# Three plain up-projection pairs in place of four, and the operands' preparation packed into six evacuations

## What is computed

```python
D_MODEL, D_FF = 1024, 2816

def swiglu(h, w_up, w_down):
    gate, up = jnp.split(h @ w_up, 2, axis=-1)
    return (jax.nn.silu(gate) * up) @ w_down

# in trunk():
h = rmsnorm(x, norm_ffn[l]) * (1.0 + sc2) + sh2
x = x + g2 * swiglu(h, w_up[l], w_down[l])
```

## Time and profile before

| | |
|---|---|
| runs, us | 939.48, 940.05, 941.44; median 940.05 |
| profiled execution, us | 940.5 |
| its span in the profile, us | 938.7 |
| granted TensorE clock | 0.995 of full speed (2.4 GHz) |
| busy, us | PE 915.1, PEld 887.8, DVE 672.3, ACT 446.5, POOL 107.6 |

### The profile page before, as it was taken

How to read it: one execution, slowest core, us unless ns; L and a number is a source line. 1 busy time by engine, 2 the same in 40 slices (tenths; PEclk the granted TensorE clock), 3 DMA queues, 4 the chain that set the end, 5 groups by cost and what they waited for, 6 DMA issues and landing times.

```text
span 938.7 us, 22364 instructions
## 1 busy us (share of the span) xinstructions
PE 915.1 (97%) x9385; PEld 887.8 (95%) x9385; DVE 672.3 (72%) x1254; ACT 446.5 (48%) x824; POOL 107.6 (11%) x135
## 2 busy tenths in 40 slices
PE   5999999999999999999999999999999999999997
PEld 4899988998999999999999999999999999999996
DVE  4778878866567677477766888999334999994454
ACT  6687445423334544753223257466213666663223
POOL 0110011112020110100100002122001322220000
PEclk8999999999999999999999999999999999999999
DMA  9834233443343422325643332332323433323212
GB/s 348 272 83 141 60 98 112 117 128 108 111 119 103 124 86 69 102 61 177 195 144 93 91 90 69 90 91 79 93 86 105 113 111 92 91 80 101 85 51 96
DMA packets 146030, 104.80 MB, mean 112 GB/s; under 512 B 5153, under 2 KB 138855, under 8 KB 144779
## 3 DMA queue, kind: packets, MB, share of 16 engines
q1 hardware_dynamic: 138955, 79.16, 28.8%
q0 software_dynamic: 6352, 22.00, 7.5%
q10 hardware_dynamic: 624, 2.23, 0.7%
HBM read 100.06 MB, written 3.31 MB: 110 GB/s over the span
## 4 chain that ended last, share of the span: by engine, by line
PE 90%; ACT 3%; DVE 3%; issue 2%; DMA 1%; SPq 1%; ACTq 0%; DVEq 0%
PE G L2225 59%; PE G L2320 19%; PE R L2233 10%; PE R L2236 1%; DMA wada<-in_w_ada_s 1%; SPq L1112 1%; DVE acc L1858 0%; DVE w_sum L1761 0%; DVE sum_lo L1770 0%; ACT L1244 0%; ACT L1283 0%; ACT inp L1283 0%; ACT w_hi L1267 0%; ACT rn L1295 0%; DVE cy L1893 0%
## 5 line engine op out<-in xcount | busy, mean ns | idle before, releaser
L2225 PE MATMUL G<-h_hi,w_hi 128*128 128x272 f32 (+1 forms) x880 | 263.4, 299 | 0.9 <-DVE w_lo L1654 0.7
L2225 PE MATMUL G<-h_lo,w_hi 128*128 128x272 f32 (+1 forms) x880 | 253.8, 288 | 0.0
L2225 PE MATMUL G<-h_hi,w_lo 128*128 128x272 f32 (+1 forms) x880 | 253.4, 288 | 0.0
L1654 DVE TENSOR_TENSOR w_lo<-raw,w_hi 128x1024 fp32r<-128x1024 f32 (+3 forms) x111 | 118.7, 1070 | 81.6 <-ACT w_hi L1267 80.5
L2225 PEld LDWEIGHTS G<-h_hi,w_hi 128*128 128x128 f32 x880 | 165.7, 188 | 4.2 <-issue 1.1
L2225 PEld LDWEIGHTS G<-h_lo,w_hi 128*128 128x128 f32 x880 | 166.0, 189 | 0.2 <-issue 0.2
L2225 PEld LDWEIGHTS G<-h_hi,w_lo 128*128 128x128 f32 x880 | 165.7, 188 | 0.0
L1267 ACT ACTIVATE w_hi<-raw 128x1024 fp32r<-128x1024 f32 (+3 forms) x111 | 101.5, 914 | 113.9 <-PE G L2225 113.6
L2320 PE MATMUL G<-x_hi,sum_hi 128*128 128x272 f32 x288 | 83.7, 291 | 1.5 <-ACT partial L1378 1.5
L2320 PE MATMUL G<-x_hi,sum_lo 128*128 128x272 f32 x288 | 83.4, 290 | 0.0
L2320 PE MATMUL G<-x_lo,sum_hi 128*128 128x272 f32 x288 | 83.1, 288 | 0.0
(11 more groups left out here) (335 smaller groups left out, 2111.7 us busy)
## 6 DMA issues: line engine op xcount, KB each, us to landing
raw<-in_w_in SPq DMA_DIRECT2D x48, 512.0 KB, 4.0
raw<-in_w_up SPq DMA_DIRECT2D x44, 512.0 KB, 3.9
w_ada<-in_w_ada_t POOLq DMA_DIRECT2D x49, 256.0 KB, 3.0
wada<-in_w_ada_s SPq DMA_DIRECT2D x8, 1024.0 KB, 13.4
raw<-in_w_down SPq DMA_DIRECT2D x14, 384.0 KB, 3.4
raw<-in_w_down SPq DMA_DIRECT2D x16, 320.0 KB, 3.1
raw<-in_w_out SPq DMA_DIRECT2D x8, 512.0 KB, 4.0
w_ada_t<-in_w_ada_t POOLq DMA_DIRECT2D x15, 256.0 KB, 3.2
```

Source lines behind the costliest of these rows:

```text
L1654: dve.tensor_tensor(lo, raw[:, i % RAW, 0:job.nk, 0:job.m], hi.bitcast(F32), ALU.subtract).then_inc(w_lo_done, 1)
L2225: ins = pe.matmul(out, w, x, start=(job.first and k == 0 and p == 0), stop=(job.last and k == job.nk - 1 and p == 2))
```

## The change

`PLAIN` becomes 3: tile 3 is made by a unit, the first run has seven units (tiles 3 to 9), and there are nineteen in all. The plain jobs have six evacuations in place of eight, and the preparation of the activation operands and of the first unit's weights is distributed over them anew. What no longer goes there, the high part of `T4` and the low parts of `B21` and `T4`, goes into the first unit's `rest`.

```diff
--- before.py
+++ after.py
@@ -54,7 +54,7 @@
 PACK = 2 * N_CHUNK
 LAST_SMALL = 4
 STAGES = 4
-PLAIN = 4
+PLAIN = 3
 PART = 10
 KP = KD // 2
 DOWN_K = (KF - PART) // 2
@@ -451,12 +451,10 @@
     rest = {n: [] for n in range(len(evac))}
     sums, high, low = prepare(0)
     rest[0] = [("x_hi", B11)]
-    rest[1] = [("x_sum", NT2), ("x_lo", B11), ("up_mul", 0)]
-    rest[2] = [("x_hi", NT1), ("x_shift", B21), ("x_sum", T3), ("x_lo", NT1), ("x_hi", B22)]
-    rest[3] = [("up_mul", 1), ("x_hi", NT2), ("x_sum", T4), ("x_lo", B22), ("x_hi", T3)]
-    rest[4] = [("x_hi", B21), ("x_lo", NT2), ("x_lo", T3), ("x_hi", T4)]
-    rest[5] = [sums[0], ("up_mul", 2), sums[1], ("x_lo", B21), *sums[2:]]
-    rest[6] = [*high[1:], ("x_lo", T4), low[0]]
+    rest[1] = [("x_sum", NT2), ("x_lo", B11), ("up_mul", 0), ("x_hi", NT1)]
+    rest[2] = [("x_shift", B21), ("x_sum", T3), ("x_lo", NT1), ("x_hi", B22), ("x_hi", NT2), ("x_lo", B22)]
+    rest[3] = [("up_mul", 1), ("x_sum", T4), sums[0], ("x_lo", NT2), sums[1], ("x_hi", T3), *sums[2:]]
+    rest[4] = [*high[1:], ("x_hi", B21), ("x_lo", T3), low[0]]
     del plan[mark:]
     plan.append(("duo", u0, u0 + 1))
     for n, one in enumerate(evac):
@@ -475,7 +473,7 @@
         if n + 2 < len(evac):
             plan.append(("split_lo", i))
         plan.extend(rest[n])
-    quick_run(range(PLAIN, PART), [("up_mul", PLAIN - 1), *low[1:]])
+    quick_run(range(PLAIN, PART), [("x_hi", T4), ("x_lo", B21), ("up_mul", PLAIN - 1), *low[1:], ("x_lo", T4)])
     for m in range(KD):
         add("down_a", m, [dict(w=t["w_down"][k0 * P:(k0 + nk) * P, m * P:(m + 1) * P].rearrange("(k p) m -> p k m", p=P),
                                nk=nk, src="a", k0=k0) for k0, nk in ((0, PART // 2), (PART // 2, PART // 2))])
```

## The result

| | before | after |
|---|---|---|
| median of 12 runs, us | 940.15 | 942.97 |
| lowest to highest | 937.59 to 943.02 | 942.01 to 946.29 |
| profiled execution, its span | 940.5, 938.7 | 944.08, 942.3 |

The medians are 2.8 us apart; the ratio is 1.0040, 95% interval 1.0029 to 1.0051, which is 3.8 us (2.7 to 4.8): slower, by more than the 0.2% that can be told apart. The runs of after lie in two groups, seven from 942.01 to 942.99, which hold the median, and five from 944.08 to 946.29, of which the profiled one is the lowest. Forecast were 942.5, a range of 940.4 to 944.7, and slower with a chance of 0.57. So it came out as forecast, but one of the terms was too small and one wasn't thought of; the rows show both.

What follows compares the result with a forecast made beforehand. TensorE is full overall, but DVE, preparing operands, ends last around the first unit. Saving - 1.43, old losses - 2.0, first unit + 5.0, later units + 0.9 give + 2.5 us: 942.5, range 940.4 to 944.7.

Steps and rivals of the forecast that it cites:

- Saving: On TensorE, a pair of 96 matmuls becomes a unit of 84: 12.14 less 10.71, 1.43 us saved.
- DVE ends last: Around the first unit, DVE finishes last and TensorE waits for it; DVE busy over 90% between 572 and 600.
- The rule weighed in the prediction: Whole kernel: work first on the engine with highest occupancy, TensorE; the sum would end at - 1.43 us.
- Three places: First unit's first product waits for `w_lo`, fifth for `sum_lo` of the third sum, seventh for `partial`; unit 14 to 16 us.
- The walk along DVE's queue: From 571.61 to the first unit's seventh product: start at 599.4 to 601.2, taken as 600.3, a 5.0 us loss.
- Wait (1): Fifth job's weights: DVE waits 0.58 us for ACT's `w_hi`, which comes later because `x_hi` is rounded first.
- wait (3): DVE's wait of 1.45 us at 603.01 stays, as ACT still rounds the last pair's result ahead of that sum.
- Wait (2): At `x_lo` of `B22`: DVE waits 1.17 us for ACT; POOL's two early sums fall largely there, minus 1.83.
- Later units: Units after the first in the first run: their old losses of 1.05 and 0.73 us half stay, 0.9.
- The packing also cures the old waits: First run of units: early sums and ready activations leave no waits; - 3.4 us, 936.6; chance 0.04.
- TensorE bounds after all: First run of units: old losses of 2.0 us stay and 1.43 is saved; 938.6; chance 0.06.
- A heavy loss: First units: DVE's waits mostly stay, later units lose as before; + 3.5 to + 5.6 us; chance 0.12.

Runs made afterwards that it cites:

- e5_four: Kernel before, four plain pairs kept, with six steps moved: four of ScalarE's and two VectorE low parts; median 937.75 us, ratio 0.9979.
- e1_read: Changed kernel with ScalarE's copy for the first unit's seventh product ahead of rounding the next unit's second sum; median 943.88 us, ratio 1.0037.
- e7_first: Changed kernel with `x_sum` of `T4` and `x_lo` of `NT2` moved behind the first unit's weights' low part; median 943.77 us, ratio 1.0048.
- e6_zero: Changed kernel with POOL filling the second unit's two sums with a constant in place of adding weights; median 941.05 us, ratio 1.0015.
- e2_act: Changed kernel with four ScalarE steps moved ahead of the last plain pair's rounding, which waits for VectorE's multiplication; median 942.22 us, ratio 1.0025.
- e4_dve: Changed kernel with all four sums of weights of each unit added on VectorE, none on POOL; median 953.17 us, ratio 1.0136.

## Why the prediction was right, and where not

**Saving: right in size.** 96 and 84 matmuls as before; settled units take 10.71 to 10.72. It was outweighed, as forecast. (10.71 was read as a unit without waits; e5_four has units of 10.58 and 10.56, so a settled one still holds some 0.14 us.)

**DVE ends last: right.** It was forecast busy over 90% between 572 and 600. The window before, then after:

```profile
571.61:600.00 28.39, 28.39 (x227) 28.39 (x226) 25.79 (x35) 17.56 (x26) 3.53 (x2) 1.00 0.26 75
571.61:600.00 28.39, 23.59 (x182) 22.76 (x180) 26.51 (x32) 18.10 (x30) 6.27 (x4) 1.00 0.26 75
```

that is 93%. As a sign this is weak, since before had 91% there; what tells are the waits on DVE's steps (rows above, e1_read, e7_first). The rule weighed in the prediction (the Trainium skill, Perfetto Trace Analysis, Identifying the Most-Contended Engine) gave 938.6; the trace disagrees here with the rule taken by the shares of the whole kernel, since they don't hold in these 30 us.

**Three places: right.** The first product starts 0.10 us after `w_lo` ends (DVE, 585.82 + 1.22), the seventh 0.10 after `partial`. For the fifth the forecast named `sum_lo` of the third sum (ends at 594.55); the row names ACT's `partial` (594.62). Both come behind the same multiplication, and the trace doesn't tell which of the two it was. The first unit took 15.94 us, forecast 14 to 16.

**The walk along DVE's queue: right in sum, not in its parts.** The seventh product was to start at 600.3 (599.4 to 601.2, before's clock); it started at 600.22 + 0.87 = 601.09, a loss of 5.81 in place of 5.0. Wait (1) was forecast 0.58 and was 0.52; wait (3), forecast 1.45, was 1.24. Wait (2), 1.17, is not there: the step that failed is "fall largely into wait (2): minus 1.83". POOL's two early sums fell on DVE's two `x_lo` at 573.33, which took 3.57 in place of 2.48, and filled the wait by stretching the work. That error came to little: - 0.66 (1.17 - 1.83) was forecast, and with 0.16 more at the `w_lo` of 572.04 it was 1.25 - 1.83 = - 0.58. The mis-sized term is the collisions in the first unit, "0 to 1.83", of which the forecast time took half, 0.9: they were 1.06 at the multiplication and 1.09 at `w_sum` (not at `w_lo`, as I had it), 2.15. e6_zero shows that they count. The corrected walk ends at 601.3, 0.2 late.

**The clock: not thought of.** It cost 1.28 us of the seventh product and 0.2 behind it, in no term and no rival.

**Later units:** 0.54 (10.75, 11.20, 10.72, against 10.71; 0.2 of it is the clock), forecast 0.9. **Second run: costed at nothing, and small:** two waits (0.37 at 742.09, 0.54 at 802.08) that before didn't have make its units 0.54 us longer in all; from its start to the end of the span after takes 0.3 longer (214.63 and 214.33).

The sum of the stretch by these rows: - 1.43 - 2.0 + 5.81 + 1.28 + 0.54 = + 4.20; the trace has 4.17. The sum on record was + 2.5. The medians say + 2.8, the ratio + 3.8 with an interval from 2.7, above the sum. That the forecast time was so near is thus partly luck: the profiled execution of after took 1.1 us more than the median, and its stretch shows 1.3 more than the medians' difference. For e7_first, where the clock fell too, stretch and medians agree (3.97 and 3.94); for e1_read they differ by 1.3 again. Whether the clock falls in every execution isn't seen in times alone, and stays open.

**Rivals.** "The packing also cures the old waits" and "TensorE bounds after all" are out. "A heavy loss" (+ 3.5 to + 5.6) is not: the profiled execution's stretch lies in it, and so does the ratio's + 3.8, while the medians' + 2.8 is the forecast case. Its mechanism was another, though: of DVE's 4.54 us of waits 1.87 are left up to `w_sum` (26.68 less 24.81 busy, from 570.73 to 597.41), and the later units lost 0.54 in place of 1.78; the collisions and the clock made the loss.

## What to carry to other kernels

A saving on the engine that is busy 97% of the kernel bought nothing here, in a stretch where another engine feeds it with what it must finish first; ask what time that stretch had, and how much of it the change takes away. Before removing work, look whether the waits that are there come from the order of a queue: here six moved steps in the kernel before gave 2.1 us, more than the 1.43 that the change spared. And when a wait is taken away, look for it one product further on: it went where the feeding engine had idled in it (e2_act) or got less to do (e6_zero), and came back where that engine was only late (e1_read, e7_first).

## What the hardware showed unexpectedly

**The clock falls within a kernel whose TensorE is busy 97% of its span.** It fell to the lower level for some 3 us in after, e1_read, e4_dve and e7_first, within 0.5 us behind a wait of 2.56, 3.58, 2.31 and 2.54 us, and was full again while the matmuls went on. The windows of e4_dve and e7_first:

```profile
599.50:602.60 3.10, 3.10 (x16) 3.10 (x16) 2.88 (x7) 1.06 (x2) 0.00 (x0) 0.50 0.02 5
599.30:602.40 3.10, 3.10 (x16) 3.10 (x15) 2.88 (x7) 1.58 (x3) 0.00 (x0) 0.50 0.02 5
```

The length of that last wait doesn't decide alone: in e2_act it was 2.60 and the clock stayed full. In the same unit in front of it e7_first had waits of 2.04 and 0.93 us, after of 1.50 and 1.54; e2_act of 1.50 alone. What makes the difference the runs don't settle.

**A constant fill by POOL did not hold DVE up.** It took 0.53 us beside a multiplication of 0.91 (e6_zero), where an addition of 1.33 us by POOL made it 1.96 (after).
